# A two-block transformer on one core: the second input's projection moved into norms 2 and 3, and the forgetting attention by pairs of heads

## The chip, the cores and the metric

One core of a Trainium2 chip runs the whole program in one launch. The metric is the device time of that launch in microseconds. PE is TensorE, DVE VectorE, ACT ScalarE, POOL GpSimd, SP SyncE (here the queue that loads the weights).

## The reference

Two blocks over 256 tokens of width 1024, all in float32. The parts that matter here, cut from the reference:

```python
def rmsnorm_2(x, w):
    y = xf * lax.rsqrt(jnp.mean(xf * xf, axis=-1, keepdims=True) + EPS)
    return (y * w)
...
def forgetting_attention(q, k, v, log_f):          # 8 heads of 64
    c = jnp.cumsum(log_f, axis=1).transpose(0, 2, 1)
    for blk in range(s // Q_BLOCK):                # two query tiles of 128
        logits = einsum('bhqd,bhkd->bhqk', q[q0:q1], k[:q1]) * scale
        logits = logits + c[:, :, q0:q1, None] - c[:, :, None, :q1]
        prob = jax.nn.softmax(where(causal, logits, -inf), axis=-1)
        outs.append(einsum('bhqk,bhkd->bhqd', prob, v[:q1]))
...
    h = h + jnp.concatenate([o_g, o_f], axis=-1) @ w_out
    hn = rmsnorm_2(h, ffn_norm_w)
    h = h + (silu(gate) * up) @ w_down
    ple_gate = jax.nn.sigmoid(rmsnorm_2(h, ple_norm_w) @ w_ple_gate)
    h = h + ple_gate * (p @ w_ple_proj)            # p: the second input, 256 x 256
    return rmsnorm_2(h, final_norm_w)
```

The first block is a gated recurrence (mLSTM) and a feed-forward with a short convolution; the second a gated delta rule (4 heads of 128) beside the forgetting attention, a feed-forward, and the gated term of `p`. `p @ w_ple_proj` depends on nothing else that is computed.

## The kernel before, in words

**Products.** Each float32 product is three matmuls of rounded parts, high by high, high by low and low by high (`mm3`, L1797 to L1799). The weights stream in groups of 1 MB through a ring of three slots: SP loads a group into `raw` (L402, in the feed-forward loops L414), ACT rounds it to `w_hi` (`hi_until`, L640), DVE subtracts to get `w_lo` (`lo_until`, L1180), and PE counts `group_used` when it is done with it. ACT may write a slot when the group three before it has been used; SP may load when DVE has taken the low part of the group three before. The order of all groups is fixed in `plan_groups`. Activations are split the same way into `h_hi` and `h_lo`. Every engine has its own hand-written instruction stream; they meet at counting semaphores only, so an engine that waits holds up all that stands behind it in its stream.

**The order of the work.** First mixer; its output projection `mix_out`; norms post1 and norm2; feed-forward `up` (11 pairs of groups in a loop) and `down`; post2 and norm3; the second block's projections `gdn` (with convolutions) and `fox`; the delta rule's triangular inversion with the attention woven in; `att_out`; norm4; `gate_up`, `down2`; the product of `p` (`ple_p`, one group); norm5; `ple_g` in two halves; final norm and stores.

**A norm** (norm2, norm3; norm4 and norm5 are alike without the first of two). For each of the two tiles of 128 tokens: ACT squares and sums (`sum_sq`, L658), POOL makes the reciprocal root (L466, L469), DVE updates `x` (L1227), ACT sums the squares of the new `x`, POOL again, and DVE scales a diagonal by the result (`diagonal`, L1210). PE then turns and scales the tile by 8 matmuls with that diagonal (`transposed`, L1910; each is recorded as two rows). When both tiles are turned ACT rounds each of 8 feature slices to `h_hi` (L691, L689), DVE makes `h_lo`; in norm2, where a shift comes in, DVE first computes the full value (L1200) and then subtracts (L1201). The first weight group after a norm does all its matmuls by high parts first (L1884, L1885) and those by `h_lo` last (L1891).

`token_block` (L1840) multiplies both token tiles group by group; with a `tail` its last two groups are done first for tile 0, then for tile 1, so that tile 0's norm can start early (`t0_done`). `mix_out` and `down` have a tail, `down2` has none.

**The second input** is loaded on ACT's queue at norm4, turned by PE (4 transposes, L1920), copied and split by DVE and ACT during `down2`, and multiplied by the weight group `ple_p` between `down2` and norm5 (24 matmuls of 512 columns). ACT copies the result to `pgate`.

**The attention.** The inversion has six levels. At each, PE multiplies (`xs`, L2439), turns `inv` (L1920), multiplies again (`y`, L2458, last level L2456), ACT copies the results out between, DVE subtracts (L1694, last L1696). Between levels PE does a product of about 5.5 to 6 us (`fox_v`, `fox`, `z`). Of the 8 heads, one goes at each step of `fox_step`: PE's logits (L2382, 128 columns; L2383, 256 columns; 64 rows of the array), DVE's scaling and bias (L1650), POOL's mask (L472), DVE's maximum (L1656, L1657), ACT's exponential (L1021), PE's three transposes (L1920), ACT's copy (L1028), PE's output products (L2400 to L2402, 64 columns), DVE's reciprocal and scaling (L1662, L1665). One step holds the logits of head i, the transposes of head i-1 and the outputs of head i-2. The outputs land by token in `mix` and are turned later by `mix_pair(0)` and `mix_pair(1)` (8 transposes), the delta rule's half by `mix_pair(2)` and `(3)`. The final product of the inversion is L2469.

## Time and profile before

| | |
|---|---|
| median of 3 runs | 840.09 us (839.66 to 842.61) |
| the profiled execution's own time | 840.55 us |
| its span, first to last instruction | 838.5 us |
| PE busy | 796.8 us, 95% of the span |
| DVE busy | 512.4 us, 61% |
| ACT busy | 386.8 us, 46% |
| POOL busy | 96.8 us, 12% |
| mean granted TensorE clock | 0.984 |

The span is what the trace shows; the own time has 2.05 us more around it. A busy PE row covers the pipeline's tail, so neighbouring rows overlap: the distance from start to start is what a matmul costs, and an idle time before a row is given in brackets with the instruction that ended it.

### The profile page before, as it was taken

What the parts mean: (1) busy time and instruction counts of PE and PEld (TensorE: products, weight loads), DVE (VectorE), ACT (ScalarE), POOL (GpSimd) and SP (SyncE); (2) the same over time, 40 slices, a digit from 0 to 9 for tenths busy, and PEclk for the clock granted to TensorE, in tenths of its full rate; (3) what the DMA queues carried; (4) which work ended last, traced back from release to release, by engine and by line L of the source; (5) the groups of instructions that cost most, each with busy time, mean ns of one, the idle gap of its engine ahead of it and who ended that gap; (6) DMA issues with size and microseconds to landing.
All of it is one profiled execution on the core that took longest, in us unless ns stands there. A gap on an engine that the chain in (4) does not pass through costs nothing. (4 is left out here: it accounts for less than half of the span.)

```text
span 838.5 us, 12695 instructions
## 1 busy us (share of the span) xinstructions
PE 796.8 (95%) x5135; PEld 711.6 (85%) x5135; DVE 512.4 (61%) x686; ACT 386.8 (46%) x527; POOL 96.8 (12%) x162
## 2 busy tenths in 40 slices
PE   4899999999799999999999999999999999999996
PEld 3578777777699999987789988988799999988885
DVE  0374789866685666685577884454464554554364
ACT  3433413544565555524367545546364344343373
POOL 3010221311100000000160314110000000000000
PEclk9899999999999999999979999999999999999999
DMA  9936577723166646587633342211455565555521
GB/s 327 382 127 216 170 258 261 274 78 100 51 201 201 196 159 193 170 291 247 200 104 102 125 131 97 102 51 55 146 189 182 172 199 184 168 175 194 182 101 50
DMA packets 102445, 142.74 MB, mean 170 GB/s; under 512 B 6263, under 2 KB 62080, under 8 KB 102400
## 3 DMA queue, kind: packets, MB, share of 16 engines
q1 hardware_dynamic: 96688, 138.42, 49.2%
q10 hardware_dynamic: 5648, 3.69, 1.5%
q8 instruction: 31, 0.51, 0.2%
q14 instruction: 14, 0.11, 0.0%
q0 software_dynamic: 64, 0.01, 0.0%
HBM read 141.05 MB, written 1.05 MB: 169 GB/s over the span
## 5 line engine op out<-in xcount | busy, mean ns | idle before, releaser
L1797 PE MATMUL ps<-h_hi,w_hi 128*128 128x256 f32 x720 | 204.5, 284 | 0.9 <-DVE w_lo L1180 0.9
L1798 PE MATMUL ps<-h_lo,w_hi 128*128 128x256 f32 x720 | 203.7, 283 | 0.0
L1799 PE MATMUL ps<-h_hi,w_lo 128*128 128x256 f32 x720 | 203.7, 283 | 0.0
L1180 DVE TENSOR_TENSOR w_lo<-raw,w_hi 128x2048 fp32r<-128x2048 f32 (+1 forms) x62 | 137.5, 2226 | 64.9 <-ACT w_hi L640 64.6
L640 ACT CAST w_hi<-raw 128x2048 fp32r<-128x2048 f32 (+1 forms) x62 | 114.9, 1856 | 88.2 <-PE ps L1799 53.2
L1797 PEld LDWEIGHTS ps<-h_hi,w_hi 128*128 128x128 f32 x720 | 138.2, 192 | 1.1 <-DVE w_lo L1180 1.1
L1188 DVE TENSOR_TENSOR w_lo<-raw,w_hi 128x2048 fp32r<-128x2048 f32 x44 | 100.8, 2290 | 61.6 <-ACT w_hi L648 61.6
L1798 PEld LDWEIGHTS ps<-h_lo,w_hi 128*128 128x128 f32 x720 | 138.2, 192 | 0.0
L1799 PEld LDWEIGHTS ps<-h_hi,w_lo 128*128 128x128 f32 x720 | 138.2, 192 | 0.0
L648 ACT CAST w_hi<-raw 128x2048 fp32r<-128x2048 f32 x44 | 83.6, 1900 | 50.6 <-PE ps L1799 50.6
L1797 PE MATMUL ps<-w_hi,h_hi 128*128 128x512 f32 x200 | 81.1, 405 | 1.2 <-DVE h_lo L1203 0.7
L1798 PE MATMUL ps<-w_lo,h_hi 128*128 128x512 f32 x200 | 78.7, 393 | 0.0
L1799 PE MATMUL ps<-w_hi,h_lo 128*128 128x512 f32 x200 | 78.6, 393 | 0.0
L1797 PE MATMUL ps<-w_hi,act_hi 128*128 128x512 f32 x176 | 69.0, 392 | 0.0
L1799 PE MATMUL ps<-w_hi,act_lo 128*128 128x512 f32 x176 | 68.5, 389 | 0.0
L1798 PE MATMUL ps<-w_lo,act_hi 128*128 128x512 f32 x176 | 68.5, 389 | 0.0
L1797 PEld LDWEIGHTS ps<-w_hi,h_hi 128*128 128x128 f32 x200 | 37.8, 189 | 11.2 <-DVE h_lo L1203 1.6
L1799 PEld LDWEIGHTS ps<-w_hi,h_lo 128*128 128x128 f32 x200 | 38.0, 190 | 8.3
L1798 PEld LDWEIGHTS ps<-w_lo,h_hi 128*128 128x128 f32 x200 | 38.0, 190 | 7.3
L1798 PEld LDWEIGHTS ps<-w_lo,act_hi 128*128 128x128 f32 x176 | 33.1, 188 | 7.0 <-issue 0.2
L1799 PEld LDWEIGHTS ps<-w_hi,act_lo 128*128 128x128 f32 x176 | 33.0, 188 | 7.0
L1797 PEld LDWEIGHTS ps<-w_hi,act_hi 128*128 128x128 f32 x176 | 33.0, 188 | 6.9 <-issue 0.2
(384 smaller groups left out, 1251.3 us busy)
## 6 DMA issues: line engine op xcount, KB each, us to landing
raw<-in_ffn_up_w SPq DMA_DIRECT2D x22, 1024.0 KB, 5.1
raw<-in_w_gate_up SPq DMA_DIRECT2D x22, 1024.0 KB, 5.1
raw<-in_ada_w SPq DMA_DIRECT2D x16, 1024.0 KB, 5.3
raw<-in_w_in SPq DMA_DIRECT2D x14, 1024.0 KB, 5.3
raw<-in_m_in_w SPq DMA_DIRECT2D x11, 1024.0 KB, 5.2
raw<-in_ffn_down_w SPq DMA_DIRECT2D x10, 1024.0 KB, 5.1
raw<-in_w_down SPq DMA_DIRECT2D x10, 1024.0 KB, 5.0
raw<-in_m_out_w SPq DMA_DIRECT2D x4, 1024.0 KB, 5.3
```

The costliest lines, as they stand in the source:

```text
L640: act.copy(part_view(w_hi, s), raw_view(split[s])).then_inc(hi_ready, 1)
L648: act.copy(part_view(w_hi, s), raw_view(split[s])).then_inc(hi_ready, 1)
L1180: dve.tensor_tensor(part_view(w_lo, s), raw_view(split[s]), part_view(w_hi, s).bitcast(F32), ALU.subtract).then_inc(lo_ready, 1)
L1188: dve.tensor_tensor(part_view(w_lo, s), raw_view(split[s]), part_view(w_hi, s).bitcast(F32), ALU.subtract).then_inc(lo_ready, 1)
L1797: pe.matmul(dst, l_hi, r_hi, start=first, stop=False)
L1798: pe.matmul(dst, l_hi, r_lo, start=False, stop=False)
L1799: return pe.matmul(dst, l_lo, r_hi, start=False, stop=last)
```

## The change

**The product of `p` moves.** The group `ple_p` leaves the weight ring. ACT's queue loads `p` (256 KB) and the left half of its weights (512 KB) as soon as the first mixer's last slices are rounded, the right half after norm2's sums. PE turns `p` before the second half of `mix_out`. ACT and DVE make the high and low parts in their post1 streams (DVE between the update of `x` and the diagonal of tile 0), those of the right half at the head of `down`. `transposed("norm2")` and `transposed("norm3")` do one half of the product each (12 matmuls) between their two tiles. ACT copies each half out (`p_store`), the first before its first step of `up`, the second after the third `gdn` evacuation, and sends it to the output tensor in HBM; it is loaded back to `pgate` at norm4. Six waits go with it: PE for the parts before each half and for the copies before the banks' next use (second step of `up`, `to_tokens(1, 1)`), ACT for the first store before the second copy, and ACT for both stores before `token_squares(0)`.

**Norms.** In norm2 ACT computes the full values of slices 4 to 7 (`full_T`) and DVE only subtracts there. `down` has a tail of three groups in place of two, and the low part of the first `gdn` group is made after tile 0's diagonal. Banks change so that the fillers have room; the first waits on `conv2_done` in `gdn` move from `gdn_tiles(2)` and `(3)` to `decay_sums` and `forget_sums(0)`.

**Norm5 by tile.** `down2` gets a tail of two groups. Tile 0 is turned between tile 1's last two groups, its slices are rounded by tile (128 columns, 16 instructions on each of ACT and DVE in place of 8 of 256), and the first half of `ple_g` runs for tile 0 while tile 1 is normalized.

**The attention by pairs of heads.** One logits step does both heads of a pair, alternating between rows 0 to 63 and 64 to 127 of the array and between banks 0 and 1. The scale goes into the evacuation of q. DVE adds the bias for both heads in two instructions, POOL masks both heads' blocks in two, ACT takes the exponential of each of the four rows, DVE divides the probabilities by their sums before they are turned, ACT copies both heads at once. The outputs are computed already turned: `fox_v` is the stationary operand (64 columns of the array for each head), the turned probabilities move (256 and 128 columns), so `mix_pair` runs twice in place of four times. The pairs' steps stand at these levels: logits 0 before level 0, logits 1, 2 and 3 in levels 1, 3 and 4, transposes after levels 0, 1 and 3 and in level 5, outputs in levels 1, 2 and 4 and after level 5. POOL's masks and level products change places to match.

The diff, cut to its core (ACT's and POOL's parts, then DVE's, then PE's):

```diff
+                blocks = logit[:].rearrange("p h (a n) -> p h a n", n=P)
+                for a in (0, 2):
+                    keep(blocks[:, :, a, :], ALU.is_ge, [[0, 2], [-1, P]], 1, fill=NEG).then_inc(S("logit_masked"), 1)
...
+            def p_weights_hi(n):
+                act.wait_ge(S("last_in"), 48 + 16 * n)
+                if n:
+                    act.wait_ge(S("p_mm"), n)
+                act.copy(pw_hi[:], pw_raw[n]).then_inc(S("pw_step"), 1)
+            def p_weights_in(n):
+                load(pw_raw[n], I["w_ple_proj_2"][0][:, n * NB:(n + 1) * NB].rearrange("(k p) n -> p k n", p=P), "last_in")
...
+            def p_store(n):
+                act.wait_ge(S("p_mm"), n + 1)
+                if n:
+                    act.wait_ge(S("p_stored"), 16 * n)
+                for t in range(TT):
+                    act.copy(p_out[:, t, :], ps[:, 2 * n + t, :]).then_inc(S("p_out"), 1)
+                act.wait_ge(S("p_out"), TT * (n + 1))
+                act.dma_start(p_rows(n), p_out[:]).then_inc(S("p_stored"), 16)
...
+            def full_T(name, banks, scale, shift):
+                for k in range(KD // 2, KD):
+                    act.activation(full[:, k, :], ps[:, banks[k // 2], k % 2 * T:(k % 2 + 1) * T], ACT.Identity,
+                                   scale=scale(k), bias=shift(k)).then_inc(S("full_ready"), 1)
...
+            def p_parts():
+                act.wait_ge(S("p_step"), 1)
+                act.copy(p_hi[:], ps[:, 0, :].rearrange("p (k t) -> p k t", k=2)).then_inc(S("p_step"), 1)
+                p_weights_hi(0)
...
+            def fox_exp(i):
+                act.wait_ge(S("fox_max"), i + 1)
+                for h in range(2):
+                    for t, part in ((0, slice(0, P)), (1, slice(P, 3 * P))):
+                        act.activation(logit[:, h, part], logit[:, h, part], ACT.Exp, bias=row_max[:, t, h:h + 1],
+                                       accum_out=row_sum[:, t, h:h + 1]).then_inc(S("prob2_ready"), 1)
+            def prT_out(i):
+                act.wait_ge(S("prT_mm"), i + 1)
+                act.copy(prT[:], ps[:, 0:2, 0:3 * P]).then_inc(S("prT_ready"), 1)
+            def fox_hi_out(i):
+                act.wait_ge(S("fox_mm"), i + 1)
+                if i == 0:
+                    act.wait_ge(S("k_dec_ready"), 1)
+                act.copy(fox_hi[:, i, :], ps[:, 2, 0:T]).then_inc(S("fox_hi_ready"), 1)
...
+            def tile_hi(t):
+                for k in range(KD):
+                    act.wait_ge(S("tr"), base("tr", "norm5") + 2 * t + k // 4 + 1)
+                    act.activation(h_hi[:, k, t * P:(t + 1) * P], tile_bank(t, k), ACT.Copy, scale=pcol("ple_norm", k))\
+                        .then_inc(S("hi"), 1)
+            hi_until(at["ple_g"][0] + 1)
+            for t in range(TT):
+                norm_half("norm5", 12, t, t, 0)
+            norm_half("norm5", 12, 2, 0, 1)
+            hi_until(at["ple_g"][0] + 2)
+            tile_hi(0)
+            norm_half("norm5", 12, 3, 1, 1)
+            hi_until(at["ple_g"][0] + 3)
+            tile_hi(1)
...
+            def p_parts():
+                dve.wait_ge(S("p_step"), 2)
+                lo_part(p_lo[:], ps[:, 0, :].rearrange("p (k t) -> p k t", k=2), p_hi[:], "p_step")
+                p_weights_lo(0)
...
+            def fox_logits(i):
+                dve.wait_ge(S("logit_mm"), i + 1)
+                blocks = ps[:, 0:2, 0:3 * P].rearrange("p h (a n) -> p h a n", n=P)
+                rows = logit[:].rearrange("p h (a n) -> p h a n", n=P)
+                c = neg_c[:, 2 * i:2 * i + 2, :]
+                dve.tensor_tensor(rows[:, :, 0:2, :], blocks[:, :, 0:2, :], c[:, :, 0:P].unsqueeze(2).to_broadcast([P, 2, 2, P]),
+                                  ALU.add)
+                dve.tensor_tensor(rows[:, :, 2, :], blocks[:, :, 2, :], c[:, :, P:T], ALU.add).then_inc(S("logit_ready"), 1)
...
+            def fox_normed(i):
+                dve.wait_ge(S("prob2_ready"), 4 * (i + 1))
+                link(dve.reciprocal(fsum[:, 1, :], fsum[:, 1, :]))
                 for t, part in ((0, slice(0, P)), (1, slice(P, 3 * P))):
+                    ins = dve.tensor_tensor(logit[:, :, part], logit[:, :, part],
+                                            row_sum[:, t, :].unsqueeze(2).to_broadcast([P, 2, (t + 1) * P]), ALU.mult)
+                ins.then_inc(S("rows_normed"), 1)
+            def fox_lo_out(i):
+                dve.wait_ge(S("fox_hi_ready"), i + 1)
+                lo_part(fox_lo[:, i, :], ps[:, 2, 0:T], fox_hi[:, i, :], "fox_done")
...
+            fox_logits(0)
+            fox_max(0)
+            update(0)
+            fox_normed(0)
+            lo_until(at["fox_v"][0] + 4)
+            fox_logits(1)
+            fox_lo_out(0)
+            fox_max(1)
+            update(1)
+            fox_normed(1)
+            lo_until(at["fox"][2] + 3)
+            fox_lo_out(1)
+            update(2)
+            lo_until(at["fox"][3] + 3)
+            fox_logits(2)
+            fox_max(2)
+            update(3)
+            fox_normed(2)
+            lo_until(at["z"][0] + 3)
+            fox_logits(3)
+            fox_max(3)
+            fox_lo_out(2)
+            update(4)
+            fox_normed(3)
+            lo_until(A0 + 2)
+            update(5)
             def mix_lo(i):
...
+            residual(0, 0)
+            residual(0, 1)
+            lo_until(at["ple_g"][0] + 1)
+            dve.wait_ge(S("t0_done"), base("t0_done", "down2") + 1)
+            residual(1, 0)
+            diagonal("norm5", 0, base("rstd", "norm5") + 1)
+            lo_until(at["ple_g"][0] + 2)
+            dve.wait_ge(group_used, at["down2"][1] + 6)
+            residual(1, 1)
+            tile_lo(0)
+            diagonal("norm5", 1, base("rstd", "norm5") + 2)
+            lo_until(at["ple_g"][0] + 3)
+            tile_lo(1)
...
                     for i, source in enumerate(sources):
-                        for s in (last - 1, last):
+                        for s in range(last + 1 - tail_groups, last + 1):
                             weights(s)
                             ins = token_group(s, g0, nk, source, ready)
                             if i == len(sources) - 1:
                                 ins.then_inc(group_used, 1)
+                                if s == last - 1 and middle is not None:
+                                    middle()
...
+            def tile_turned(t):
+                pe.wait_ge(S("diag"), base("diag", "norm5") + t + 1)
+                for k in range(KD):
...
+            def p_product(n):
+                pe.wait_ge(S("p_step"), 3)
+                pe.wait_ge(S("pw_step"), 2 * (n + 1))
                 for t in range(TT):
+                    for k in range(2):
+                        tok = slice(t * P, (t + 1) * P)
+                        ins = mm3(ps[:, 2 * n + t, :], (p_hi[:, k, tok], p_lo[:, k, tok]), (pw_hi[:, k, :], pw_lo[:, k, :]),
+                                  k == 0, k == 1)
+                ins.then_inc(S("p_mm"), 1)
...
+            def fox_logits(i):
+                for t, part, keys in ((0, slice(0, P), slice(0, P)), (1, slice(P, 3 * P), slice(0, T))):
+                    for h in range(2):
+                        row = slice(FD * h, FD * h + FD)
+                        ins = pe.matmul(ps[:, h, part], foxT[row, i, t * P:(t + 1) * P], foxT[row, FP + i, keys],
+                                        start=True, stop=True)
+                ins.then_inc(S("logit_mm"), 1)
...
+                for s in range(TT):
+                    for h in range(2):
+                        c = slice((2 * i + h) * FD, (2 * i + h + 1) * FD)
+                        ins = pe.matmul(ps[FD * h:FD * h + FD, 2, s * P:T], fox_v[:, s, c], prT[:, h, 2 * P * s:2 * P + s * P],
+                                        start=s == 0, stop=s == 1)
+                ins.then_inc(S("fox_mm"), 1)
...
+                if i in (3, 4):
+                    fox_logits(i - 1)
...
-                fox_step(FOX_STEPS[i][0])
+                if i == 5:
+                    fox_transpose(3)
+                elif i in (1, 2, 4):
+                    fox_out(i // 2)
+                    if i == 1:
+                        fox_logits(1)
...
-                if FOX_STEPS[i][1] is not None:
-                    fox_step(FOX_STEPS[i][1])
+                if i in (0, 1, 3):
+                    fox_transpose((i + 1) // 2)
+            fox_out(3)
...
```

## Rows read from the trace of the kernel before

**Rows 1.** Page, first part: engine, busy us, share of the span, instructions.

```profile
PE 796.8 (95%) x5135; PEld 711.6 (85%) x5135; DVE 512.4 (61%) x686; ACT 386.8 (46%) x527; POOL 96.8 (12%) x162
```

**Rows 2.** Stretches: us; busy us of PE, PEld, DVE, ACT, POOL; clock; DMA share, GB/s.

```profile
221.00:224.50 3.50, 3.44 (x18) 3.45 (x19) 1.10 (x3) 2.75 (x6) 0.00 (x0) 0.58 0.00 0
433.30:484.40 51.10, 50.65 (x429) 49.96 (x426) 41.07 (x73) 33.56 (x55) 10.36 (x15) 1.00 0.45 145
499.10:575.70 76.60, 74.74 (x525) 66.97 (x525) 39.42 (x82) 38.01 (x76) 18.17 (x23) 1.00 0.23 79
799.80:830.70 30.90, 30.86 (x153) 25.83 (x151) 19.99 (x26) 18.76 (x33) 2.68 (x6) 1.00 0.12 44
```

**Rows 3.** Timeline of PE, norm2: start, us, instruction, idle before.

```profile
215.70 2.05 PE L1910 MATMUL ps<-diag,x 128*128 128x128 f32 x16 [0.33 <-DVE diag L1210]
221.06 3.41 PE L1910 MATMUL ps<-diag,x 128*128 128x128 f32 x16 [3.30 <-DVE diag L1210]
...
233.04 0.39 PE L1797 MATMUL ps<-h_hi,w_hi 128*128 128x256 f32 x1 [0.86 <-DVE w_lo L1180]
```

**Rows 4.** Timeline of ACT, then of DVE, norm2.

```profile
219.67 1.90 ACT L640 CAST w_hi<-raw 128x2048 fp32r<-128x2048 f32 x1
222.32 3.76 ACT L691 ACTIVATE h_hi<-ps,mod 128x256 fp32r<-128x256 f32 x8 [0.75 <-PE ps L1910]
...
223.37 0.55 DVE L1200 TENSOR_SCALAR full<-ps,mod 128x256 f32<-128x256 f32 x1 [2.37 <-ACT h_hi L691]
223.95 0.42 DVE L1201 TENSOR_TENSOR h_lo<-full,h_hi 128x256 fp32r<-128x256 f32 x1
```

**Rows 5.** Timeline of PE, norm3.

```profile
417.88 3.26 PE L1910 MATMUL ps<-diag,x 128*128 128x128 f32 x16 [2.00 <-DVE diag L1210]
423.04 3.78 PE L1910 MATMUL ps<-diag,x 128*128 128x128 f32 x16 [1.90 <-DVE diag L1210]
```

**Rows 6.** Timeline: ACT's last of five DMA issues and DVE's gate part, norm3; ACT, norm4.

```profile
423.38 0.46 ACTq L651 DMA_DIRECT2D gprm<-in_fox_f_bias  x1
...
429.72 0.44 DVE L1192 TENSOR_TENSOR wg_parts<-wsm,wg_parts 128x128 fp32r<-128x128 f32 x1 [1.11 <-ACT wg_parts L900]
...
611.18 3.03 ACT L689 ACTIVATE h_hi<-ps,cols 128x256 fp32r<-128x256 f32 x8 [0.25 <-PE ps L1910]
```

**Rows 7.** Timeline of PE: first matmul of the product of `p`, and norm5.

```profile
799.71 0.39 PE L1797 MATMUL ps<-w_hi,p_hi 128*128 128x512 f32 x1
...
805.15 3.73 PE L1910 MATMUL ps<-diag,x 128*128 128x128 f32 x32
```

**Rows 8.** Timeline of DVE, norm5: the updates of `x`, the first diagonal.

```profile
801.39 1.28 DVE L1238 TENSOR_TENSOR x<-x,ps 128x512 f32<-128x512 f32 x2
803.97 0.29 DVE L1210 TENSOR_SCALAR diag<-ident,rstd 128x128 f32<-128x128 f32 x1 [1.30 <-POOL rstd L469]
```

**Rows 9.** Timeline in `down`: the low part of its second half's first group; its first matmul.

```profile
381.14 2.29 DVE L1180 TENSOR_TENSOR w_lo<-raw,w_hi 128x2048 fp32r<-128x2048 f32 x1 [1.51 <-ACT w_hi L640]
...
384.04 0.39 PE L1797 MATMUL ps<-w_hi,act_hi 128*128 128x512 f32 x1
```

**Rows 10.** Timeline of PE, one attention step of the third level.

```profile
517.83 0.48 PE L2382 MATMUL ps<-foxT 64*128 64x128 f32 x2
...
518.68 0.55 PE L1920 MATMUL ps<-ident,r 128*128 128x128 f32 x3
519.06 0.33 PE L2400 MATMUL ps<-fox_v,r 128*128 128x64 f32 x2
...
519.67 0.55 PE L2458 MATMUL ps<-og,r 128*128 128x128 f32 x3
```

**Rows 11.** Timeline of PE: four matmuls in four 32-column parts of the array.

```profile
21.60 1.06 PE L1941 MATMUL ps<-gp,cpad 128*32 128x512 f32 x8
```

**Rows 12.** Groups of POOL from 494 to 580 us: count; busy us, mean ns; idle.

```profile
L598 POOL TENSOR_TENSOR cTl<-cT,level 128x1024 f32<-128x1024 f32 x6 | 14.3, 2387 | 18.2 <-DVE cT L1625 16.5 <-PE ps L2439 1.7
L472 POOL TENSOR_SCALAR_AFFINE_SELECT r<-r 128x128 f32<-128x128 f32 x16 | 4.4, 294 | 47.4 <-DVE r L1650 47.3
```

More of the change, by code:

```diff
@@ L154, in two_blocks @@
                      ("final", 2)),
-            "t0_done": (("mix_out", 1), ("down", 1), ("att_out", 1), ("ple_g", 1)),
+            "t0_done": (("mix_out", 1), ("down", 1), ("att_out", 1), ("down2", 1), ("ple_g", 1)),
             "diag": (("norm1", 4), ("norm2", 2), ("norm3", 2), ("norm4", 2), ("norm5", 2)),
@@ L162, in two_blocks @@
         for kind, n in (("tr", KD // 2), ("hi", KD), ("hT", KD)):
-            FAMILY[kind] = (("norm1", KD), ("y1", n), ("norm2", n), ("norm3", n), ("mix", KD // 2), ("norm4", n),
+            FAMILY[kind] = (("norm1", KD), ("y1", n), ("norm2", n), ("norm3", n), ("mix", 2), ("norm4", n),
                             ("norm5", n))
@@ L955, in _ @@
             gdn_mid(2, ahead=False)
+            p_store(1)
             for t in range(TT):
@@ L1840, in token_block @@
-            def token_block(g0, sources, nk=KD, after_first=None, ready=None, free=None, done=None, tail=None,
-                            split_of=None):
+                    pe.wait_ge(S("hi"), base("hi", "norm5") + t * KD + k + 1)
+                    pe.matmul(ps[:, bank, :], h_hi[:, k, tok], hi[:, j, :], start=k == 0, stop=False)
+                    pe.matmul(ps[:, bank, :], h_hi[:, k, tok], lo[:, j, :], start=False, stop=False)
+                for j in range(4):
+                    k = 4 * (s - g0) + j
+                    pe.wait_ge(S("hT"), base("hT", "norm5") + t * KD + k + 1)
+                    ins = pe.matmul(ps[:, bank, :], h_lo[:, k, tok], hi[:, j, :], start=False, stop=k == KD - 1)
@@ L1845, in token_block @@
+                return ins
+            def token_block(g0, sources, nk=KD, after_first=None, ready=None, free=None, done=None, tail=None, middle=None,
+                            tail_groups=2):
                 last = g0 + (nk + 3) // 4 - 1
-                together = range(g0, last - 1 if tail else last + 1)
+                together = range(g0, last + 1 - tail_groups if tail else last + 1)
                 for s in together:
                     weights(s)
-                    if split_of is not None:
-                        high_parts(s, g0, sources, split_of)
```

464 lines of the change are left out of this document (205 added, 259 removed).

## The prediction

> **What bounds the kernel now.** I read the page's busy times first: PE is busy 796.8 us, 95% of the span, DVE 61% and ACT 46% [rows 1]. Only two things can shorten such a kernel: fewer matmul columns in series, and the PE's idle time. So the second view is PE's own waits, and after it the timelines around them. In norm2 PE turns tile 0, is idle 3.30 us, turns tile 1, and starts in steady state only at 233.04, after a last wait of 0.86 us for a low part [rows 3]. The eight matmuls of a turned tile take 2.05 us at full clock; behind the idle 3.3 us they take 3.41, and the granted clock of that stretch is 0.58, a mixture of 2.4 and 1.2 GHz [rows 2, 3]. In norm3 it is idle 2.00 and 1.90 us, and both tiles take 3.26 and 3.78 us, again the lower level [rows 5]. Three more stretches matter for how well they are filled: 433 to 484 us, with 50.65 of 51.10 us busy, the attention, with 1.86 us idle in 76.6, and the last stage, 30.86 busy of 30.90 [rows 2].
>
> **Norm2.** The filler is half of the product of p: all 24 matmuls take 5.44 us, so 12 take 2.72 [rows 7]. Tile 0's transposes end at 217.7, the filler at 220.5, tile 1's diagonal comes at 221.0 as before [rows 3]: PE idles 0.6 us in place of 3.30, and I expect the clock to stay at 2.4 GHz, so tile 1 takes 1.9 and not 3.2 us start to start. The parts for it I cost at nothing. ACT's two (about 1.6 us, scaled by columns from its 1.90 us cast, [rows 4]) stand in front of `t0_done`, for which it waits. DVE's two (0.7 + 1.15, the second from half of a group's 2.29 us, [rows 9]) stand between the update of x and the diagonal. There the sums of two halves and POOL keep DVE waiting about 2 us: one half's chain is 2.2 us already [rows 8]. Without that cover they would cost 1.85. ACT finishes a rounding at 221.57 and can then do its eight slices at 0.38 us each (3.03 for eight in norm4, [rows 6]; 3.76 now, held up by PE), until 224.7, then four full values until 226.2. DVE does slices 0 to 3 at 0.96 us each and 4 to 7 at 0.42 instead of 0.96 [rows 4], so it saves 2.2 us, ends at 228.0, and has the next weights' low part ready 2.29 us later at 230.3 instead of 233.0. That is what PE waits for: **-2.7 us**, with the 2.72 us of the product inside.
>
> **Ahead of it** PE turns p: four transposes, **+0.4** (three cost 0.38 us start to start, [rows 10]). It needs ACT's two loads, issued one token block of 24 matmuls earlier, that is some 5 us; I take no wait, and bound it by 0 and 1 us. **In down** the right half's parts put 1.15 us into DVE's stream. The second half's first group is low at 383.43 and wanted at 384.04 [rows 9]: slack 0.6, because each SP load waits for DVE's last step. **+0.4** (0 to 1.15).
>
> **Norm3.** The longer tail starts tile 0's chain 2.7 us earlier (four k blocks of 3 matmuls at 0.227 us), so its idle 2.00 us go. Tile 1's chain starts with `down`'s end as before and comes out about 0.7 us earlier, since DVE and ACT no longer finish tile 0 in front of it. PE has the second filler in between, and idles about 1 us. PE alone would gain 2.8 us. But ACT's slices can start only behind its five DMA issues, which end at 423.84 now [rows 6]. Those move by the 0.7 us, and the slices by another half us or so, since PE no longer turns at half clock: ACT and DVE come out some 1.4 us earlier. From the gates' low part at 429.72 [rows 6] DVE and ACT form a dense chain through the convolutions, and PE beside them has almost no slack either [rows 2]. The slower chain decides: **-1.4** (bounds 0 and -2.8). `p_store(1)` is 1.2 us of ACT; it falls where ACT waits for the decays.
>
> **The attention.** One head costs PE 0.85 us of logits, 0.38 of transposes and 0.61 of outputs, 1.84 in all [rows 10], eight heads 14.7 us. After: the six transposes of a pair cost the same 0.7. The four logits matmuls of a pair are 1.5 us in series, and the outputs have twice the columns of before, 1.4 us in series. The nearest row for their overlap: four matmuls of 512 columns in four column parts take 1.06 us, when one float32 matmul of 512 columns (two recorded rows, four passes, scaled from the 256 columns' 0.43) alone is 0.85 [rows 11]. They ran side by side. The outputs are of this kind, so 0.7 us; the logits split rows and not columns, and no row shows that; by the same row I take 0.75, and keep 1.5 as the other end. So a pair costs 2.15 us and four pairs 8.6, against 14.7: -6.1. The first logits stand where PE waits anyway, and in some levels PE now arrives ahead of ACT's four copies, which I put at 1 us given back (0 to 2). The attention's 1.86 us of idle time [rows 2] mostly goes: -1.5, and the last level gains 0.4 by order. Together **-7.0**. The eight transposes of `mix_pair` that go are **-0.9**.
>
> Each pair's softmax must hide behind PE's 5.5 to 6 us between levels. Two adds, a maximum in three steps and a division in three on DVE, four exponentials on ACT, at 0.4 to 0.7 us each by the sizes of [rows 4, 8], and POOL's four blocks at 0.294 us [rows 12] come to 6.5 us or so. But the chain starts 2 to 3 us before that product does, so the division should end 1 to 2 us before the transposes want it.
>
> The Trainium skill, in TensorEngine Tiling (Array Packing), section Tiling Modes, says that tiles of the array work in parallel, and that changing the mode drains it. By the first the logits would overlap too and the sum stands; by the second each change would cost something, and 16 changes of mode are as many as before, so it takes nothing from the sum. No row here shows row parts overlapping.
>
> **The end.** PE does the same transposes and `ple_g`, but the 5.44 us of the product are gone from it, and with them the cover of norm5 (30.86 of 30.90 busy, [rows 2]). Tile 0: from `t0_done` DVE finishes a low part (0.25), updates x (0.69), and 2.2 us later its diagonal is done, by the distance from the first half's end, 802.1, to 804.26 [rows 8]. That is 3.1 against 12 matmuls or 2.72 us: wait 0.35. The tile's transposes and tile 1's last six matmuls then stand before the first `ple_g`, while ACT rounds four slices; DVE's low slices come just in time or 0.2 us late. Tile 1's norm hides behind tile 0's 24 matmuls. 5.44 - 0.35 - 0.2: **-4.9** (bounds -5.4, and -2.0 if every slice of 128 columns costs as much as one of 256).
>
> **Sum:** -2.7 + 0.4 + 0.4 - 1.4 - 7.0 - 0.9 - 4.9 = -16.1. I give back 1.0 for waits of the kind that a walk misses; of these, before, one cost 0.33 to 0.86 us [rows 3]. From the execution's own 840.55 us that gives 825.5; the median is 840.09, 0.05% away, and I don't correct for it.
>
> **The rivals.**
> A. *The logits run in series*, or outputs too. For it: only column parts are shown side by side [rows 11]. Logits alone: +1.8 on the path, 827.3; both: 829.5.
> B. *The fillers fit, but the chains of DVE and ACT don't come out earlier*: norm3 gains nothing, the end only 2 us, a load of p is late. 825.5 + 1.4 + 2.9 + 1.0 = 830.8. For it: DVE and ACT carry more in norm2 and the end than before; against: at the end they are 65% and 61% busy [rows 2].
> C. *Slower: the softmax chain of a pair becomes the bound.* DVE's update of the inversion stands behind `fox_max`, which waits for POOL's mask, and POOL's mask can stand behind a level product of 2.39 us [rows 12]; all of PE's next level waits for that update. It decides from the point where the update ends later than PE's 5.5 us product. With product, masks and both passes exposed, 2.4 + 1.2 + 1.2 = 4.8 us at each of four pairs: +19.2, 844.7. Against: the level products stand before the masks at times when POOL is idle (18.2 us of waits in that row).
> D. *The change does less than it says*: the filler waits for its parts in both norms, so that 2 x 2.7 us lie on the path: 830.9. Against: the parts are asked for 6 us ahead in norm2 and 60 in norm3.
>
> **Chances.** Forecast 0.50 (821 to 828 as its own range), A 0.20, B 0.15, D 0.06, C 0.03; 0.06 for a gain even larger, as where PE's gain in norm3 comes through (821 to 819). What a measurement of this kernel can tell from no change is 0.5%, 4.2 us. All cases but C, and a little of B and D made worse, are faster than 835.9. The range 820.5 to 832.5 takes in A, B, D and the unknown ends of the costs.
>
> **What would show it.** After: PE's wait before tile 1 in norm2 under 1 us and both tiles of norms 2 and 3 near 2.05 us, with the clock at 1.00; two groups of 12 matmuls by `p_hi` inside the norms; the steady start of `up` 2 to 3 us nearer to `mix_out`'s end. In the attention, the starts of the two heads' logits a few hundredths of a us apart if they overlap, and some 68 us from the first `fox_v` matmul to L2469's successor where it was 76.5. From `down2`'s end to the last matmul about 26 us where it was 30.9. The forecast is wrong if PE shows waits of over 2 us at `inv_ready`, before `fox_transpose`, or at the first `ple_g` slices, or if the lower clock stays in any norm.

## The result, and the profile after

The changed kernel takes 828.47 us (median of four runs, 827.14 to 830.37), the kernel before 841.13 us on the same chip (839.66 to 842.61): a ratio of 0.9836, 95% interval 0.9802 to 0.9871. It is 12.7 us faster, inside the predicted range and 3 us above the predicted time, just outside the forecast's own narrower range of 821 to 828. The execution that was profiled took 829.55 us (span 827.6), 11.0 us less than the profiled one of before. What each engine was busy, from the top of the page of after, to be read against [rows 1]:

```profile
PE 789.4 (95%) x5111; PEld 701.8 (85%) x5111; DVE 509.3 (62%) x660; ACT 390.7 (47%) x538; POOL 96.5 (12%) x154
```

PE's busy time fell by only 7.4 us, so the sum does not yet say where the gain lies. I cut both traces at the same matmuls and compared the lengths of the stretches. A stretch runs from the start of a PE row to the start of another; where it meets the end of `mix_out`, of `down`, of `att_out` or of the program, that end is the end of the last row. `gT` is the first product of the delta rule's keys and queries, `fox_v` the first product inside the inversion, `vb` the one behind it.

| stretch, between matmuls of PE | before | after | measured | forecast |
|---|---|---|---|---|
| start to the end of `mix_out` | 215.38 | 216.54 | +1.16 | +0.4 |
| to the steady start of `up` (norm2) | 17.66 | 14.83 | -2.83 | -2.7 |
| to `down`'s first matmul | 121.05 | 121.05 | 0 | 0 |
| to `down`'s last | 61.80 | 65.69 | **+3.89** | **+0.4** |
| to the `gT` products (norm3, gdn) | 68.50 | 67.48 | -1.02 | -1.4 |
| to the first `fox_v` | 14.74 | 14.74 | 0 | 0 |
| to the `vb` product (attention) | 76.53 | 70.50 | -6.03 | -7.0 |
| to the end of `att_out` | 31.04 | 30.20 | -0.84 | -0.9 |
| to norm4's transposes | 1.57 | 1.58 | 0 | 0 |
| to `down2`'s first matmul | 131.48 | 131.13 | -0.35 | none |
| to the last matmul (end) | 90.91 | 86.11 | -4.80 | -4.9 |
| allowance for small waits | | | | +1.0 |
| sum | 830.66 | 819.85 | -10.81 | -15.1 |

One row is wrong by 3.5 us, two by about 1 us. These are PE's waits from the list of waits of after (engine, line, what it waited for: total us, times, longest), those of the stretches that changed:

```profile
PE ps L2035 <- DVE diag L1296: 4.8, 3, 2.4
PE ps L1909 <- DVE w_lo L1263: 2.2, 2, 2.0
PE ps L2416 <- ACT neg_c L996: 1.1, 1, 1.1
PE ps L2591 <- ACT r L1017: 0.7, 1, 0.7
PE ps L2012 <- DVE diag L1296: 0.4, 1, 0.4
PE ps L2593 <- ACT r L1017: 0.3, 1, 0.3
```

L2035 is the norms' transposes (9.1 us in five waits before), L2012 the new norm5 by tile, L1909 the three-part matmul. The wait of 2.0 us for `w_lo` is new, and it lies in the middle of `down`. The timeline of PE in after, at norm2 (against [rows 3]), at that wait, and at norm3 (against [rows 5]); columns: start, duration, engine, line, operation, tile, count, idle time and its releaser:

```profile
217.35 2.05 PE L2035 MATMUL ps<-diag,x 128*128 128x128 f32 x16 [0.81 <-DVE diag L1296]
219.16 0.48 PE L1909 MATMUL ps<-pw_hi,p_hi 128*128 128x512 f32 x1
...
221.76 0.39 PE L1911 MATMUL ps<-pw_hi,p_lo 128*128 128x512 f32 x1
222.22 0.49 PE L2035 MATMUL ps<-diag,x 128*128 128x128 f32 x2
...
384.51 0.50 PE L1909 MATMUL ps<-w_hi,act_hi 128*128 128x512 f32 x1 [1.99 <-DVE w_lo L1263]
...
425.00 0.49 PE L2035 MATMUL ps<-diag,x 128*128 128x128 f32 x2 [2.37 <-DVE diag L1296]
```

In norm2 the filler ends at 222.15 and tile 1's transposes start at 222.22: the idle 3.30 us are full. In norm3 2.37 us stay idle behind the filler. The stretches by time (length, busy time of each engine, granted clock, DMA share, GB/s), against [rows 2]:

```profile
217.30:224.30 7.00, 6.88 (x46) 6.05 (x47) 2.67 (x5) 4.72 (x9) 1.73 (x4) 1.00 0.26 76
384.50:391.90 7.40, 7.39 (x25) 5.98 (x26) 2.29 (x1) 3.40 (x6) 0.00 (x0) 0.77 0.84 286
438.60:485.60 47.00, 45.44 (x384) 44.87 (x383) 37.22 (x67) 30.30 (x53) 7.24 (x12) 1.00 0.46 144
500.30:570.80 70.50, 69.38 (x504) 61.71 (x504) 39.25 (x53) 39.54 (x75) 16.84 (x15) 1.00 0.27 90
788.50:819.90 31.40, 30.98 (x152) 25.50 (x150) 20.76 (x34) 17.83 (x37) 2.58 (x6) 1.00 0.10 34
```

Norm2 keeps the upper level of the clock (0.58 before). The second line is the surprise: the 24 matmuls behind the wait in `down` take 7.36 us at a mean clock of 0.77, a mixture of 2.4 and 1.2 GHz, where the same 24 took 5.6 us before. The group starts 2.1 us late and then takes 1.8 us longer: together the 3.89.

### The profile page after: what moved, and what is told of

It is laid out like the page before. It is cut to its first block and busy times, and to the rows that moved or that the text cites. A ratio compares the mean times of both kernels' runs of the same rounds, so it can differ in the third digit from the quotient of the medians.

```text
span 827.6 us, 12597 instructions
## 1 busy us (share of the span) xinstructions
PE 789.4 (95%) x5111; PEld 701.8 (85%) x5111; DVE 509.3 (62%) x660; ACT 390.7 (47%) x538; POOL 96.5 (12%) x154
## 5 line engine op out<-in xcount | busy, mean ns | idle before, releaser
L1909 PE MATMUL ps<-h_hi,w_hi 128*128 128x256 f32 x720 | 204.5, 284 | 0.2 <-DVE w_lo L1263 0.2
L1263 DVE TENSOR_TENSOR w_lo<-raw,w_hi 128x2048 fp32r<-128x2048 f32 (+1 forms) x61 | 135.3, 2225 | 62.0 <-ACT w_hi L663 61.7
L663 ACT CAST w_hi<-raw 128x2048 fp32r<-128x2048 f32 (+1 forms) x61 | 113.1, 1856 | 88.4 <-PE ps L1911 53.0
L1909 PEld LDWEIGHTS ps<-h_hi,w_hi 128*128 128x128 f32 x720 | 138.2, 192 | 0.5 <-DVE w_lo L1263 0.5
L1909 PE MATMUL ps<-w_hi,h_hi 128*128 128x512 f32 x184 | 74.8, 407 | 1.2 <-DVE h_lo L1289 0.7
L1911 PE MATMUL ps<-w_hi,h_lo 128*128 128x512 f32 x184 | 72.8, 395 | 0.0
L1910 PE MATMUL ps<-w_lo,h_hi 128*128 128x512 f32 x184 | 72.7, 395 | 0.0
L1909 PE MATMUL ps<-w_hi,act_hi 128*128 128x512 f32 x176 | 69.8, 397 | 2.0 <-DVE w_lo L1263 2.0
L1909 PEld LDWEIGHTS ps<-w_hi,h_hi 128*128 128x128 f32 x184 | 35.1, 191 | 10.7 <-DVE h_lo L1289 1.6
L1911 PEld LDWEIGHTS ps<-w_hi,h_lo 128*128 128x128 f32 x184 | 35.1, 191 | 7.7
L1909 PEld LDWEIGHTS ps<-w_hi,act_hi 128*128 128x128 f32 x176 | 33.4, 190 | 9.5 <-DVE w_lo L1263 2.4
L1910 PEld LDWEIGHTS ps<-w_lo,h_hi 128*128 128x128 f32 x184 | 35.2, 191 | 6.8
L485 POOL TENSOR_SCALAR ss<-ss 128x1 f32<-128x1 f32 x14 | 5.5, 395 | 293.2 <-ACT junk L681 293.2
```

Source lines behind the costliest of these rows:

```text
L485: link(pool.tensor_scalar(s, s, ss[:, c0 + TT:c0 + TT + 1], EPS, ALU.add, ALU.add))
L663: act.copy(part_view(w_hi, s), raw_view(split[s])).then_inc(hi_ready, 1)
L1263: dve.tensor_tensor(part_view(w_lo, s), raw_view(split[s]), part_view(w_hi, s).bitcast(F32), ALU.subtract).then_inc(lo_ready, 1)
L1909: pe.matmul(dst, l_hi, r_hi, start=first, stop=False)
L1910: pe.matmul(dst, l_hi, r_lo, start=False, stop=False)
L1911: return pe.matmul(dst, l_lo, r_hi, start=False, stop=last)
```

## The experiments

Eleven kernels ran: ten edits of the changed one, and the changed one once more. The profile of each gives the stretches. Medians stand against the kernel before on the same chip: in brackets the lowest and highest run, then the ratio to before and its 95% interval. A kernel for which only a time "in all" is given ran once, so its stretches count and its total says little. Two theories for the missing 3.5 us: the *ring* (the right half's parts at the head of `down` delay every later load), and the *loads or the longer tail*.

**The right half's parts made in `up`.**

```diff
+                if r is ROUNDS and u == 0:
+                    p_weights_hi(1)
                 hi_ahead(U0 + 4, r, u)
...
+                if r is ROUNDS and u == 0:
+                    p_weights_lo(1)
                 lo_ahead(U0 + 4, r, u)
```

> The changed kernel, with the right half's two weight parts (ACT 1.05 us, DVE 1.22 us) made in the last steps of up, where ACT waits 2.19 us for PE and DVE 1.24 us for ACT, and no longer at the head of down's ring of loads. Theory (ring): these parts are what made PE wait 1.98 us in the middle of down and then run its next 24 matmuls in 7.4 us instead of 5.5; both go, so down gets 3.9 us shorter (65.7 to 61.8 us from its first to its last matmul) and the median goes from 828.5 to about 824.6. Rival (loads): the wait comes from a load that landed 6.5 us after its issue where it took 5.2 before, or from the longer tail, and has nothing to do with the parts: wait and time stay as they are, within 1 us.

`down` took 62.46 us in place of 65.69, and the wait 0.38 instead of 1.99. The same load in the two timelines, first of after, then of this run: DVE's stream at the head of `down`, and ACT's cast of the group that PE then waited for.

```profile
357.43 1.22 DVE L1275 TENSOR_TENSOR pw_lo<-pw_raw,pw_hi 128x1024 fp32r<-128x1024 f32 x1
358.56 0.48 DVE L1241 TENSOR_SCALAR acc<-raw,cpad 128x512 f32<-128x512 f32 x1
361.44 2.29 DVE L1263 TENSOR_TENSOR w_lo<-raw,w_hi 128x2048 fp32r<-128x2048 f32 x1
...
380.15 1.91 ACT L663 CAST w_hi<-raw 128x2048 fp32r<-128x2048 f32 x1 [8.29 <-DMA raw<-in_ffn_down_w]
382.16 2.29 DVE L1263 TENSOR_TENSOR w_lo<-raw,w_hi 128x2048 fp32r<-128x2048 f32 x1 [2.87 <-ACT w_hi L663]
```

```profile
356.39 0.48 DVE L1242 TENSOR_SCALAR acc<-raw,cpad 128x512 f32<-128x512 f32 x1
359.27 2.29 DVE L1264 TENSOR_TENSOR w_lo<-raw,w_hi 128x2048 fp32r<-128x2048 f32 x1
...
377.50 1.91 ACT L663 CAST w_hi<-raw 128x2048 fp32r<-128x2048 f32 x1 [8.05 <-DMA raw<-in_ffn_down_w]
379.51 2.29 DVE L1264 TENSOR_TENSOR w_lo<-raw,w_hi 128x2048 fp32r<-128x2048 f32 x1 [2.82 <-ACT w_hi L663]
```

Counted from `down`'s first matmul (352.42 and 351.38), the first low part starts at 9.02 against 7.89, and 20 us later the cast starts at 27.73 against 26.12. That is one execution against one. In the two later versions with the parts in `up` the cast starts at 26.64 and 26.11, with waits of 0.89 and 0.36 us, and in all eight executions with the parts once at `down`'s head it starts between 27.5 and 27.8: the parts cost 0.9 to 1.7 us at the load that counts, about DVE's own time. The rest of the delay is not theirs. In the kernel before the cast came at 25.03, counted alike, from a load issued at 19.85, where it is issued at 19.80 in this run:

```profile
373.94 0.37 SPq L402 DMA_DIRECT2D raw<-in_ffn_down_w  x1
...
379.12 1.92 ACT L640 CAST w_hi<-raw 128x2048 fp32r<-128x2048 f32 x1 [6.88 <-DMA raw<-in_ffn_down_w]
```

From issue to cast it is 5.2 us there, and 6.2 to 6.6 us in all twelve executions of the changed kernel and its edits, wherever the parts, the fillers and the tail stand. The next load is issued 1.26 us behind it in both kernels. Why the load is slower stays open; there is only one profile of before. The median was 828.02 us (825.09 to 828.87; 0.9847, 0.9824 to 0.9871): the profiled execution had the expected time, the median did not show it. The stretch is shown, the gain in the median is not.

**The low part twice**, so 1.2 us more at the same place.

```diff
+            dve.wait_ge(S("pw_step"), 3)
+            link(dve.tensor_tensor(pw_lo[:], pw_raw[1], pw_hi[:].bitcast(F32), ALU.subtract))
             p_weights_lo(1)
```

> The changed kernel, with DVE's low part of the right half computed twice at the head of down's ring, so 1.2 us more in DVE's stream there. Theory (ring, each load waits for DVE's last step): PE's wait in the middle of down grows from 1.98 to about 3.2 us, down from first to last matmul from 65.7 to about 66.9 us, and more if the lower clock behind the wait lasts longer. Rival (loads or tail): the wait stays near 2 us.

The wait grew from 1.99 to 3.02 us, `down` to 66.71 (833.03 us in all). With the run before: less of DVE there 0.38, as is 1.99, more 3.02. The ring theory holds for what DVE's time adds. This execution took 3.5 us more than the profiled one of after, and the rest of it lies where nothing was changed: `mix_out` ended 1.1 us later, and the attention's stretch took 72.11 us in place of 70.50, with the same waits and a lower clock at its start:

```profile
502.30:520.00 17.70, 17.68 (x93) 15.25 (x94) 9.88 (x12) 8.10 (x16) 7.50 (x6) 0.90 0.18 60
```

**The longer tail of `down` undone** (`tail_groups=3` left out).

> The changed kernel, with two groups of four k blocks instead of three taken tile by tile at the end of down (the longer tail undone). Theory (the longer tail lets norm3's first tile hide): tile 0's diagonal comes after down's end by about 2 us, PE waits 2 us ahead of tile 0 and again up to 2 us ahead of tile 1 less what the filler covers, and down's end to the gT matmuls grows from 67.5 us by 0.5 to 2 us. Rival (DVE and ACT decide, not PE): unchanged within 0.5 us. If the longer tail also made the wait in the middle of down, that wait of 1.9 us goes; if the parts made it, it stays.

The wait in `down` stayed, at 1.78: the tail doesn't make it. `down` to `gT` grew from 67.5 to 70.90 us, more than expected: PE waited 1.54 and 3.23 us at the two tiles, and tile 1 then took 3.78 us at a clock of 0.50. The tail is worth 3.4 us, the clock behind the longer wait included. (833.9 us in all.)

**The fillers behind both tiles.**

```diff
-            transposed("norm2", lambda: p_product(0))
+            transposed("norm2")
+            p_product(0)
```

and the same for norm3.

> The changed kernel, with both halves of the product put behind the second tile's transposes of norm2 and norm3 instead of between the tiles. The same work, no filler in the gaps. Theory (the filler is worth its own time and keeps the clock): PE idles some 2.5 to 3 us again between the tiles of norm2 and over 4 us in norm3, the tile behind the gap takes 3.4 instead of 2.05 us and its granted clock falls under 0.7; the product delays the first half of up's and gdn's high slices little, since PE waits there for ACT and DVE anyway; norm2 from mix_out's end to the steady start gets 0.5 to 2.5 us longer (14.8 to about 16.5) and norm3 0 to 2. Rival (the fillers fit anywhere behind the transposes, where DVE's slices are awaited): no difference within 0.5 us in either norm. Median 828.5 to 832 by the first, 828.5 by the second.

834.63 us (831.26 to 837.53; 0.9927, 0.9901 to 0.9953). Its PE timeline in norm2, and the clock of tile 1 there and in norm3:

```profile
217.14 2.05 PE L2035 MATMUL ps<-diag,x 128*128 128x128 f32 x16 [0.80 <-DVE diag L1296]
222.00 3.60 PE L2035 MATMUL ps<-diag,x 128*128 128x128 f32 x16 [2.81 <-DVE diag L1296]
```

```profile
222.00:225.60 3.60, 3.60 (x17) 3.60 (x18) 1.25 (x3) 2.85 (x7) 0.00 (x0) 0.54 0.39 137
425.70:429.50 3.80, 3.80 (x17) 3.80 (x18) 1.67 (x4) 2.51 (x6) 3.39 (x7) 0.50 0.18 10
```

Norm2 took 17.60 us (17.66 before the change), `down` to `gT` 70.38: 2.8 and 2.9 us more than in after, above the 2.5 and 2 us that were expected at most, and the median lies above the expected 832 as well. The place of the fillers is worth about the product's own 2.72 us. The slower clock of tile 1 (3.60 and 3.79 instead of 2.05 us) hardly shows in the sum; that PE's later waits for DVE hide it is my reading, which no run took apart. The rival, that they fit anywhere, is out.

**The second half stored earlier**: `p_store(1)` ahead of ACT's wait for the softplus.

> The changed kernel, with the second half of the product taken out and stored where ACT waits 3.49 us for the softplus, and not ahead of the decays. Theory (ACT is the dense chain there): ACT and all behind it come out 1.2 us earlier, PE's wait of 1.11 us for neg_c goes, and from down's end to the gT matmuls it is 66.3 instead of 67.5 us; median about 827.3. Rival (another chain, DVE's convolutions, sets the end of that stretch): PE's wait only moves, 67.5 us stays within 0.3, median 828.5.

67.45 us from `down` to `gT`, and PE's wait for `neg_c` still 1.12: no gain (827.44 us; 0.9842, 0.9819 to 0.9866). ACT only waits longer for DVE's decays (2.19 instead of 0.86 us). DVE's chain sets this stretch, and the 1.5 us of ACT cost nothing.

**The low part behind tile 1's diagonal** in norm3, with the parts in `up`.

```diff
-                    if t == 0 and after_diagonal is not None:
-                        after_diagonal()
+                if after_diagonal is not None:
+                    after_diagonal()
```

> The changed kernel with the right half's parts made in up (as in the run before it) and, in norm3, the next weights' low part (2.29 us of DVE) put behind tile 1's diagonal and not between the two. Theory (DVE is the dense chain of the stretch, and what starts it is tile 1's diagonal, held up by that low part): the diagonal comes 1.3 to 1.9 us earlier, PE's wait of 2.35 us ahead of tile 1 falls under 1 us, and from down's end to the gT matmuls it is 65.7 to 66.2 instead of 67.4 us. Rival (ACT's five DMA issues, 2.9 us, hold its slices back anyway, or the low part only delays gdn's first tile by as much): 67.4 us within 0.5.

PE's wait went from 2.35 to 1.65 us, not under 1, and the stretch from 67.40 to 66.41: 1.0 us less, where 1.2 to 1.7 was expected. Median 825.21 us (824.51 to 825.49; 0.9807, 0.9784 to 0.983). DVE's timeline in after shows what stood there, a low part between the two tiles' updates:

```profile
416.60 0.28 DVE L1296 TENSOR_SCALAR diag<-ident,rstd 128x128 f32<-128x128 f32 x1 [1.99 <-POOL rstd L488]
417.50 2.29 DVE L1263 TENSOR_TENSOR w_lo<-raw,w_hi 128x2048 fp32r<-128x2048 f32 x1 [0.62 <-ACT w_hi L663]
419.71 0.68 DVE L1308 TENSOR_TENSOR full<-ps,gp 128x512 f32<-128x512 f32 x1
```

**The logits by head** (the loops over heads and blocks exchanged), and **the outputs by head**, one kernel each.

> The changed kernel, with the four logits matmuls of a pair issued head by head (both of head 0, then both of head 1) instead of alternating between the heads' row parts. Theory (row parts overlap): the four, now 0.85 us from their start to the next operation's, take about 1.3 to 1.5 us, of which one boundary still overlaps; over three pairs inside the attention's stretch that is 1.4 to 2 us, 70.5 to about 72. Rival A (they run in series anyway and are short for another reason): still 0.85 us, 70.5 us.

> The changed kernel, with the four output matmuls of a pair issued head by head instead of alternating between the two column parts. Theory (column parts overlap): the four, now 0.80 us from start to the next operation's start, take about 1.2 to 1.4 us, four times in the stretch: 70.5 to about 72.5 us. Rival: they stay at 0.80 us.

Neither changed anything: 70.53 us in both (828.98 and 829.88 us in all). PE's timeline, of after and of the logits by head (eight records are four float32 matmuls):

```profile
518.42 0.87 PE L2539 MATMUL ps<-r,fox_v 128*64 128x256 f32 x8
519.22 0.93 PE L2517 MATMUL ps<-foxT 64*128 64x128 f32 x8
520.07 0.38 PE L2593 MATMUL ps<-og,r 128*128 128x128 f32 x1
```

```profile
518.54 0.93 PE L2517 MATMUL ps<-foxT 64*128 64x128 f32 x8
519.41 0.38 PE L2593 MATMUL ps<-og,r 128*128 128x128 f32 x1
```

Both theories could still explain that: no overlap at all, or an overlap that needs no order. So the last run took the heads apart.

**The heads of two pairs kept apart** by the level's transposes.

```diff
-                    fox_logits(i - 1)
+                    fox_logits(i - 1, (0,))
...
+                if i in (3, 4):
+                    fox_logits(i - 1, (1,))
```

> The changed kernel, with the two heads of pairs 2 and 3 kept apart: head 0's two logits matmuls stand ahead of the level's eight transposes, head 1's two behind them, so that nothing of one head can run beside the other. Theory (the row parts of a pair run side by side, whatever the order in the program, as the run by head let one suppose): each head then costs 0.85 us of its own, as in the kernel before, so each of the two levels gets 0.85 us longer and the attention's stretch goes from 70.5 to 72.2 us. Rival (the pair is short because few columns in a row are cheap when issued back to back, and nothing overlaps): each head costs half of the pair's 0.85 us, and the stretch stays at 70.5 to 70.9 us.

The stretch took 72.17 us, and each single head as long as the pair had:

```profile
542.97 0.92 PE L2517 MATMUL ps<-foxT 64*128 64x128 f32 x4
543.82 1.09 PE L2045 MATMUL ps<-ident,r 128*128 128x128 f32 x8
544.85 0.92 PE L2517 MATMUL ps<-foxT 64*128 64x128 f32 x4
```

The two heads of a pair do run side by side. The length of the stretch alone would not show it, since 72.11 us came once without any change there; but here the clock is 1.00 all through, and the time comes at the two levels, 0.8 us at the one and 0.9 at the other. (832.63 us in all.)

**Five places at once**, and **the changed kernel again** beside it.

> The changed kernel with five instructions or pairs put elsewhere: the two of the run before it (the right half's parts in up; the low part behind tile 1's diagonal in norm3); the left half's weight parts made while the first half of mix_out runs, where DVE waits 2.9 us, and not between x and tile 0's diagonal, where POOL's operation on the sums took 0.88 us instead of 0.30 while DVE made them; ACT's second neg_c copy ahead of the last silus and not behind two squares (PE waits 1.1 us for it); ACT's rounding of att_out's second weights behind the last level's copies and not ahead of them (PE waits 0.7 us there). Theory: mix_out's end to steady start 14.8 to 14.3 us, down 62.5 to 63, down's end to gT 66.4 to 65.3, the attention's stretch 70.5 to 69.8; against the changed kernel -0.5 -2.5 -2.1 -0.7, some 5.5 us less, median about 823. Rival (each stretch is held by DVE's chain, and the waits only move): only what the run before had, 825.2.

> The changed kernel itself, once more, beside the version above on the same chip, for their comparison and for what differs between executions of one program. Expected by the stages: all of them within 0.1 us of the profile shown, except the head (up to mix_out's end, 215 to 219 us so far) and the 24 matmuls behind down's wait (7.36 us in three of six executions, 5.78 in the other three); median 828 to 829.

825.53 us (824.16 to 827.87; 0.9811, 0.9788 to 0.9834) against 828.70 (826.38 to 829.59; 0.9836, 0.9813 to 0.9859). Two of the three new places gave nothing. The left half's weights arrived only at 202.71, ACT waited 3.98 us for them, PE's wait ahead of tile 0 was 1.07 us (0.81 in after), and norm2 stayed at 14.82. With `neg_c` early, PE's wait for it went, but the stretch stayed at 66.34: PE waits 0.75 for DVE's `qk_n` and 0.78 for `gT` instead. The third, ACT's rounding behind the last copies, took 0.93 us from the attention (69.54). The gain was 3.2 us where 5.5 was expected. The changed kernel again had every stage within 0.1 us of its first profile but two: the head ended at 215.65 in place of 216.54, and `down` to `gT` took 67.79 us, with tile 1's transposes at 2.68 us. The best versions, this one and the one with two places (825.21), are some 3 us faster than the changed kernel and 16 faster than the one before.

## Why the prediction was right, and where it was off

**Norm2**, -2.7: right (-2.83), by its own steps: the filler fits, tile 1 takes 2.05 us, the clock stays at 1.00. The run with the fillers behind gave the 2.8 us back. One step was off: DVE's two parts were put at nothing, and PE's wait ahead of tile 0 grew from 0.33 to 0.81 us; the stretch came out as forecast all the same.

**`down`'s ring**, +0.4 with bounds 0 and 1.15: this is the step that failed. The mechanism was named (each load waits for DVE's last step, slack 0.6), but the price was capped at DVE's own 1.15 us. It measured 3.89. Against the run with the parts in `up`, 1.6 us are a longer wait and 1.6 us the clock of the 24 matmuls behind it; 0.66 us stays without the parts, with a wait of 0.38 (0.36 and 0.89 us in the two later versions). So DVE's time was sized nearly right (0.9 to 1.7 us at the wait). What the forecast lacked is that the load that counts took 1.0 to 1.4 us longer from issue to cast than in before, which used up the slack of 0.6, and the clock. I had priced clocks behind idle time in the norms, where the rows of before showed them, and not behind a new wait. A wait of 2 us was not in the bounds, so neither was what follows it. Why that load is slower stays open.

**Ahead of norm2**, +0.4: the four transposes cost 0.41 us. The other 0.8 us can't be put down to the change: the eleven further executions came to this point between 215.2 and 219.3 us, and of before there is one profile alone. That their removal in front of `down2` gives 0.35 back was left out of the sum.

**Norm3**, -1.4: -1.02. That the slower of DVE's and ACT's chains decides was right; it was DVE's, and ACT's store, which I had asked a place for, costs nothing. What I had missed is the 2.29 us low part between the diagonals: PE idled 2.37 us ahead of tile 1, not about 1. "Wrong if the lower clock stays in any norm" was one of the signs: in this profile it is gone, but behind the same wait tile 1 took 2.68 us in the changed kernel's other trace.

**Attention**, -7.0: -6.03. A pair costs 0.65 (transposes), 0.80 (outputs) and 0.85 us (logits), 2.30 in place of 2.15: 0.6 us over four pairs. The idle time fell from 1.86 to 1.12 us, not by 1.5. The two make 1.3 us of a miss of 0.97; the 1 us given back and the 0.4 of the last level were not taken apart. That row parts overlap like column parts was the choice made without a row; the run with the heads apart bears it out, and rival A is wrong for the logits. Its price was too low as well: apart, a pair costs 0.85 us more, 2.6 us for the three pairs in the stretch, not 1.8. The outputs weren't taken apart; but one head's two matmuls have the 256 and 128 columns of one head's logits, which take 0.85 us alone, and both heads' outputs together took 0.80. `mix_pair`, -0.9: -0.84. The softmax of a pair stays hidden (the longest wait of PE left in the stretch is 0.72 us), so rival C is wrong too.

**The end**, -4.9: -4.80, with a wait of 0.36 us at tile 0's diagonal where 0.35 was forecast. Rival B (the chains don't come out earlier) is wrong at the end and mostly so in norm3; rival D (the filler waits for its parts) is wrong: there is no wait ahead of either filler.

**The allowance** of 1.0 us hid part of the miss. Without it the sum was -16.1 against -10.8. The range of 12 us held the result because it also took in rivals that turned out wrong: 828.47 lies nearer to rival A's 827.3 than to the forecast's 825.5, though A is wrong. The stretches show the mechanism right; that the total fell in the range is no proof of it.

## What to carry to other kernels

In a ring of loads where each load waits for an engine's last step, work put at the ring's head comes back at a later load, here 20 us later and at about its own length. Ask how much slack the *tightest* later group has, don't trust 0.6 us of it from a single trace, and add the clock that PE can lose behind the new wait, here as much again. Work for another purpose belongs where its engine waits for PE, not where PE will wait for it. Filling PE's idle stretch with real work is worth its full length; beside it, look for an operation of another engine that stands between two tiles' chains only because the program says so.

## What the runs showed of the hardware

The order of the matmuls in the program didn't matter for their overlap. With the logits by head, head 1's first block stands behind head 0's second, which has to wait for head 0's first: in strict order that is 0.32 us and then head 1's own 0.85, some 1.17 us by [rows 10]. It took 0.87. (The trace shows when records start, not their place in the program; that the order of the program reached the engine as written is taken for granted here.) PE's timeline of that run, the four logits cut three ways (a row has the shape of its first record):

```profile
518.54 0.50 PE L2517 MATMUL ps<-foxT 64*128 64x128 f32 x4
518.56 0.70 PE L2517 MATMUL ps<-foxT 64*128 64x128 f32 x5
518.87 0.61 PE L2517 MATMUL ps<-foxT 64*128 64x256 f32 x4
```

The two records that start at 518.54 and 518.56 are the first blocks of both heads, and the blocks of 256 columns come behind them, from 518.87. The Trainium skill, in TensorE: Matmul & The Clock Gate, section The mechanism, says that weight loads are pulled ahead but matmuls start and end strictly in order. For these float32 matmuls on two row parts the measured 0.87 us speaks against it. Its other statement there, that matmuls on different parts run at once, agrees with the run that kept the heads apart.

The clock behind a wait differs between executions. In `down` five with waits of 1.92 to 2.02 us ran the next 24 matmuls in 7.3 to 7.4 us, and three with 1.78, 1.80 and 1.89 us ran them in 5.78; these waits are not equal, so these rows alone don't show chance. The windows of the run with the store moved show one of the three, to be read beside the clock of 0.77 above:

```profile
383.10:388.80 5.70, 5.70 (x25) 4.70 (x26) 2.29 (x1) 3.33 (x6) 0.00 (x0) 1.00 0.83 287
```

Norm3 shows it: behind an equal wait of 2.35 to 2.37 us the eight transposes took 2.05 us in four executions and 2.68, 2.82, 2.97 and 3.27 in four others. There it costs little, since PE's later wait for `neg_c` shrinks (from 1.11 to 0.58 and 0.21 us in two of them) and `down` to `gT` stays at 67.4 to 67.8 us. At the attention's start it cost 1.6 us once, behind waits of 0.6 and 0.5 us. Such draws can be part of the 3 us by which executions of one program differ; the head, which ended between 215.2 and 219.3 us, is a larger part.

POOL's small operation on the sums took 0.88 us instead of 0.30 in after, while DVE made the left half's low part, and tile 0's diagonal, which waits for it, came later (PE's wait 0.81 us, before 0.33 [rows 3]). Its rows, in after and in the version with five places, where that part is made earlier:

```profile
215.44 0.88 POOL L485 TENSOR_SCALAR ss<-ss 128x1 f32<-128x1 f32 x1 [2.54 <-ACT junk L681]
```

```profile
216.15 0.30 POOL L485 TENSOR_SCALAR ss<-ss 128x1 f32<-128x1 f32 x1 [3.39 <-ACT junk L681]
```

The Trainium skill, in GPSIMD Engine Reference, section Specifications, says that POOL shares its SBUF interfaces with VectorE and meets contention when DVE's instruction has two SBUF inputs. The low part is of that kind (`pw_raw` and `pw_hi`), and these rows agree. It looks like more than a slow-down: POOL's operation on the sums meets such a low part three more times in after, and in all four cases it ends within 0.2 us behind DVE's instruction, however long that still has to run. At its longest:

```profile
194.27 2.34 POOL L487 TENSOR_SCALAR ss<-ss 128x2 f32<-128x2 f32 x1 [4.68 <-ACT junk L681]
...
194.27 2.28 DVE L1263 TENSOR_TENSOR w_lo<-raw,w_hi 128x2048 fp32r<-128x2048 f32 x1
```

In norm3 it took 1.02 us beside the low part between the two tiles, and DVE waited 0.32 us for its result before it updated tile 1. Beside DVE's `full`, which reads one input from PSUM, it stays at 0.30. Moving the part away did not pay in norm2: in the version with five places PE waited 1.07 us ahead of tile 0.
